# Seven block products in place of eight in three of four rounds of a feed-forward matrix

## The reference

```
x += m @ w_out
x += relu(RMSNorm(x) * g_mlp @ w_up)^2 @ w_down       # w_up 1024 x 4096, w_down 4096 x 1024
y = RMSNorm(x) * g_final                              # the meta tokens are dropped
```

## Time and profile before

| | |
|---|---|
| median of 3 runs | 953.61 us (953.61 to 954.35) |
| the profiled execution, its own time | 954.1 us |
| its span, first to last instruction | 952.3 us |
| TensorE busy | 941.3 us, 7473 matmuls |
| VectorE, ScalarE, GpSimd busy | 535.3, 528.7, 257.3 us |
| mean granted TensorE clock | 0.999 |

### The profile page before, as it was taken

How to read it: one execution, slowest core, us unless ns; L and a number is a source line. 1 busy time by engine, 2 the same in 40 slices (tenths; PEclk the granted TensorE clock), 3 DMA queues, 4 the chain that set the end, 5 groups by cost and what they waited for, 6 DMA issues and landing times.

```text
span 952.3 us, 19721 instructions
## 1 busy us (share of the span) xinstructions
PE 941.3 (99%) x7473; PEld 923.1 (97%) x7473; DVE 535.3 (56%) x915; ACT 528.7 (56%) x826; POOL 257.3 (27%) x188
## 2 busy tenths in 40 slices
PE   8999999999999999999999999999999999999997
PEld 8899999999999999999999999999999999999997
DVE  6479999999999999997653322222111122221133
ACT  6788787878787878786733343333111133331153
POOL 5301010101010101012243444445334244454340
PEclk9999999999999999999999999999999999999999
DMA  6776667676758585768132223234233133243102
GB/s 181 151 175 132 171 125 176 121 180 116 185 109 184 109 181 113 158 144 211 46 110 80 80 85 101 85 93 120 89 88 89 47 88 88 88 121 98 45 23 95
DMA packets 189520, 111.37 MB, mean 117 GB/s; under 512 B 35437, under 2 KB 181277, under 8 KB 189482
## 3 DMA queue, kind: packets, MB, share of 16 engines
q1 hardware_dynamic: 176666, 80.28, 30.6%
q0 software_dynamic: 7632, 27.79, 15.9%
q10 hardware_dynamic: 5184, 2.78, 1.0%
HBM read 75.97 MB, written 7.06 MB: 87 GB/s over the span
## 4 chain that ended last, share of the span: by engine, by line
PE 97%; ACT 1%; DMA 1%; issue 1%; DVE 0%; POOL 0%; DVEq 0%; POOLq 0%
PE dense L551 83%; PE z L671 3%; PE dense L846 3%; PE z L635 2%; PE z L705 2%; DMA w_lo<-w_raw 1%; PE z L565 1%; PE z L639 1%; PE dense L715 0%; PE z L838 0%; PE z L629 0%; PE dense L578 0%; PE z L691 0%; PE z L710 0%; PE z L621 0%
## 5 line engine op out<-in xcount | busy, mean ns | idle before, releaser
L534 POOL TENSOR_TENSOR w_lo<-w_raw,w_hi 128x1024 fp32r<-128x1024 f32 x80 | 192.3, 2406 | 295.0 <-ACT w_hi L939 295.0
L551 PE MATMUL dense<-r_hi,w_hi 128*128 128x272 f32 (+1 forms) x1264 | 263.5, 291 | 1.2 <-DMA w_lo<-w_raw 0.6
L551 PE MATMUL dense<-r_lo,w_hi 128*128 128x272 f32 (+1 forms) x1264 | 262.6, 289 | 0.0
L551 PE MATMUL dense<-r_hi,w_lo 128*128 128x272 f32 (+1 forms) x1264 | 262.2, 289 | 0.0
L939 ACT ACTIVATE w_hi<-w_raw 128x1024 fp32r<-128x1024 f32 x134 | 140.9, 1054 | 113.6 <-PE dense L551 102.6
L551 PEld LDWEIGHTS dense<-r_hi,w_hi 128*128 128x128 f32 x1264 | 198.2, 188 | 1.6 <-DMA w_lo<-w_raw 0.8
L551 PEld LDWEIGHTS dense<-r_lo,w_hi 128*128 128x128 f32 x1264 | 198.8, 188 | 0.7 <-DVE r_lo L1355 0.6
L551 PEld LDWEIGHTS dense<-r_hi,w_lo 128*128 128x128 f32 x1264 | 199.1, 188 | 0.0
L1374 DVE SCALAR_TENSOR_TENSOR acc<-conv_in,cw_cur,acc 128x574 f32<-128x574 f32 x232 | 172.8, 811 | 0.5
L511 POOL DMA_DIRECT2D w_lo<-w_raw x53 | 45.2, 853 | 362.4 <-ACT w_lo L941 362.4
L551 PE MATMUL dense<-s_hi,w_hi 128*128 128x272 f32 x640 | 132.3, 288 | 0.0
(11 more groups left out here) (258 smaller groups left out, 1289.6 us busy)
## 6 DMA issues: line engine op xcount, KB each, us to landing
w_raw<-in_w_in_dram SPq DMA_DIRECT2D x54, 512.0 KB, 5.5
w_lo<-w_raw POOLq DMA_DIRECT2D x53, 512.0 KB, 5.0
w_raw<-in_w_up_dram SPq DMA_DIRECT2D x32, 512.0 KB, 4.0
w_raw<-in_w_down_dram SPq DMA_DIRECT2D x32, 512.0 KB, 3.5
w_raw<-in_w_pw_dram SPq DMA_DIRECT2D x8, 512.0 KB, 3.6
w_raw<-in_w_out_dram SPq DMA_DIRECT2D x8, 512.0 KB, 3.6
x_tok<-in_x_prompt_dram SPq DMA_DIRECT2D x4, 512.0 KB, 6.1
out_dram<-k_blk SPq DMA_DIRECT2D x32, 64.0 KB, 2.4
```

The source lines that it names most:

```text
L534: pool.tensor_tensor(w_lo[:, n], w_raw[:, n], w_hi[:, n].bitcast(F32), ALU.subtract).then_inc(lo_post, 1)
L551: mm = nc.tensor.matmul(out[:, h, 0:half], w[:, wslot, k, :], m[:, k, c0 + h * half:c0 + (h + 1) * half], start=(k == 0 and n == 0), stop= ...
```

## The change

In rounds 0, 1 and 2 the down product of 1024 inner channels by 1024 outputs is made by Strassen's scheme on blocks. Output chunks are taken in pairs (4 pairs a round); inner chunks too: A11, A12, A21, A22 are the quarters of the weights of one pair (even or odd inner chunks, first or second output chunk), B11, B12, B21, B22 those of the activations (even or odd inner chunk, first or second 272 tokens). In place of eight block products there are seven (`SEVEN`), each with 4 inner chunks x 3 passes = 12 matmuls of 272 columns into one bank, with sums of blocks as operands: S1 to S4 of the weights, T1 to T4 of the activations. For that

- the rounds are no longer taken two by two: each has 8 up units and then its down part. Round 3 keeps the plain form, with its up results in `u_hi`, `u_lo`. There are 16 groups in place of 22.
- VectorE makes the sums S1 to S4 (128 x 512 each, in what was `gate_c`), four for each pair of outputs; the first pair's between the up units 5 and 6 of its round, the others between the additions of the pair before.
- ScalarE makes the high parts: of the quarters A11, A12, A22, which it also copies negated into `w_lo`, and of the sums. Each waits until TensorE has finished with the same form of the pair before, for each form has one place in `w_hi` and `w_lo`.
- GpSimd makes the low parts: for the three quarters by an accumulating DMA from `w_raw` (a source of four pieces of 512 B in each partition), for the four sums by a subtraction of 128 x 512.
- the up units of these rounds are turned into seven forms (B11, T1 after an even unit, B21, B22, T2, T3, T4 after an odd one), high parts on ScalarE, sums and low parts on VectorE, in `r_hi`, `r_lo`, `u_hi`, `u_lo`.
- VectorE adds the four bank results x, y, z, w to `xT` in nine additions of 272 columns for each pair (`add_product`). Pairs take `dense` and `z` in turn. TensorE starts product S2 after the addition x11, S3 after x12, A22 after z11.
- SP loads the two blocks of a pair when the pair two before has its low parts and its sums.

```diff
-N_GROUPS = (3 + 2 * ROUNDS) * GROUPS_PER_STAGE
+
+N_SEVEN = ROUNDS - 1
+N_GROUPS = (3 + ROUNDS + 1) * GROUPS_PER_STAGE
+PAIRS = KC // 2
+PRODUCTS = 7
...
+        FORM_HOME = {"A11": (0, 0), "A12": (0, 1), "S1": (1, 0), "S2": (1, 1), "S4": (2, 0), "S3": (2, 1), "A22": (3, 0)}
+        QUARTER_FORMS, SUM_FORMS = ("A11", "A12", "A22"), ("S1", "S2", "S4", "S3")
+        U_FORMS = ("B11", "T1", "B21", "B22", "T2", "T3", "T4")
+        U_SUMS = ("T1", "T2", "T3", "T4")
+        SEVEN = (("A11", "B11", 0, True), ("S1", "T1", 1, True), ("A12", "B21", 2, True), ("S2", "T2", 0, False),
+                 ("S4", "B22", 3, True), ("S3", "T3", 0, False), ("A22", "T4", 2, True))
+        MADE = {w: n + 1 for n, (w, _, _, _) in enumerate(SEVEN)}
+
+        ADDED = {"x11": 1, "z11": 2, "x12": 3, "y12": 4, "w12": 5, "x22": 6, "x21": 7, "y22": 8, "z21": 9}
+        N_ADDED = len(ADDED)
+
+        def form_place(buf, name):
+            slot, h = FORM_HOME[name]
+            return buf[:, slot, h * PAIRS:(h + 1) * PAIRS, :]
+
+        def quarter(P_, name):
+
+            slot = 2 * (P_ % 2) + (name[1] == "2")
+            return w_raw[:, slot].rearrange("p (k t) c -> p t k c", t=2)[:, int(name[2]) - 1]
+
+        def wsum(name):
+            at = OUTTOK + SUM_FORMS.index(name) * PAIRS * P
+            return gate_c[:].rearrange("p k c -> p (k c)")[:, at:at + PAIRS * P].rearrange("p (k c) -> p k c", c=P)
...
+        def u_form(name, m, low=False):
+            n = U_FORMS.index(name)
+            buf = ((r_hi, r_lo), (u_hi, u_lo))[n // 4][low]
+            return buf[:].rearrange("p k c -> p (k c)")[:, ((n % 4) * PAIRS + m) * HALFO:((n % 4) * PAIRS + m + 1) * HALFO]
+
+        def product_bank(P_, n):
+            return z[:, n, 0:HALFO] if P_ % 2 else dense[:, n % 2, n // 2, 0:HALFO]
...
+            def seven_left(P_, b):
+
+                if b == 0:
+                    sync.wait_ge(quarter_lo[0], 16 * (P_ + 1))
+                    sync.wait_ge(quarter_lo[1], 16 * (P_ + 1))
+                else:
+                    sync.wait_ge(quarter_lo[2], 16 * (P_ + 1))
+                sync.wait_ge(wsum_done, len(SUM_FORMS) * (P_ + 1))
...
+                        P_ = PAIRS * rr + p
+                        for b in range(2):
+                            slot = 2 * (p % 2) + b
+                            if p < 2:
+                                sync.wait_ge(lo_post, lows_of_post(g0 + 1, slot))
+                            else:
+                                seven_left(P_ - 2, b)
+                            sync.dma_start(w_raw[:, slot], wdown_v[:, rr, :, 2 * p + b, :]).then_inc(raw_seven[slot], 16)
...
+            def seven_low(P_):
+
+                for name, _ in sorted(MADE.items(), key=lambda item: item[1]):
+                    if name in QUARTER_FORMS:
+                        f = QUARTER_FORMS.index(name)
+                        pool.wait_ge(quarter_hi, len(QUARTER_FORMS) * P_ + f + 1)
+                        pool.dma_start(form_place(w_lo, name).bitcast(F32), quarter(P_, name), accum_op=ALU.add).then_inc(quarter_lo[f], 16)
+                    else:
+                        pool.wait_ge(wsumhi_done, len(SUM_FORMS) * P_ + SUM_FORMS.index(name) + 1)
+                        pool.tensor_tensor(form_place(w_lo, name), wsum(name), form_place(w_hi, name).bitcast(F32), ALU.subtract).then_inc(wsumlo_done, 1)
...
+            def seven(rr, p):
+                P_ = PAIRS * rr + p
+                if p == 0:
+                    for slot in range(2):
+                        claim(slot, X_EMPTIED[slot] + 2 * up_group(rr + 1))
+                if P_ >= 2:
+                    pe.wait_ge(product_added, N_ADDED * (P_ - 1))
+                for name, moving, b, begin in SEVEN:
+                    if name in QUARTER_FORMS:
+                        pe.wait_ge(quarter_lo[QUARTER_FORMS.index(name)], 16 * (P_ + 1))
+                    else:
+                        pe.wait_ge(wsumlo_done, len(SUM_FORMS) * P_ + SUM_FORMS.index(name) + 1)
+
+                    before = {"S2": "x11", "S3": "x12", "A22": "z11"}.get(name)
+                    if before:
+                        pe.wait_ge(product_added, N_ADDED * P_ + ADDED[before])
+                    if p == 0 and name == "A11":
+                        pe.wait_ge(form_ready, form_count(rr, PAIRS - 2, U_FORMS[-1]))
+                    hi, lo = form_place(w_hi, name), form_place(w_lo, name)
+                    for m in range(PAIRS):
+                        if p == 0 and m == PAIRS - 1:
+                            pe.wait_ge(form_ready, form_count(rr, m, moving))
+                        for j, (w, low) in enumerate(((hi, False), (hi, True), (lo, False))):
+                            mm = nc.tensor.matmul(product_bank(P_, b), w[:, m, :], u_form(moving, m, low),
+                                                  start=(begin and m == 0 and j == 0), stop=(m == PAIRS - 1 and j == 2), skip_group_check=True)
+                    mm.then_inc(product_done, 1)
...
+            for rr in range(ROUNDS):
+                g0 = up_group(rr)
+                if rr > 0:
+                    pe.wait_ge(product_added, N_ADDED * (PAIRS * rr - 1))
+                with pe.Fori(g0 + 1 if rr == 0 else g0, g0 + 2) as g:
                     group(g, s_hi, s_lo)
-                with pe.Fori(10 + 8 * rr, 12 + 8 * rr) as g:
-                    group(g, *u_parts[0], (u_ready, 16 * rr + 1))
-                if rr == 0:
-                    with pe.Fori(12, 14) as g:
-                        group(g, *u_parts[1], (u_ready, KC + 1))
-                else:
-                    for f in range(4):
-                        unit(20, f, *u_parts[1], (u_ready, 3 * KC + 1) if f == 0 else None)
-                        if f >= 1:
-                            pe.wait_ge(xg_done, f)
-                            back(f - 1, ((0, 0), (1, 1), (2, 2), (3, 3)))
+                if rr < N_SEVEN:
+                    for p in range(PAIRS):
+                        seven(rr, p)
+            pe.wait_ge(product_added, N_ADDED * PAIRS * N_SEVEN)
+            for f in range(4):
+                unit(LAST_GROUP - 1, f, u_hi, u_lo, (u_ready, 1) if f == 0 else None)
...
+                if rr < N_SEVEN:
+                    m = f // 2
+                    halves = [n32[:, n % 2, h * HALFO:(h + 1) * HALFO] for h in range(2)]
+                    if n % 2 == 0:
+                        nc.scalar.activation(u_form("B11", m), halves[0], ACT.Copy).then_inc(form_hi, 1)
+                        u_sum_high(rr, m, "T1")
+                    else:
+                        nc.scalar.activation(u_form("B21", m), halves[0], ACT.Copy).then_inc(form_hi, 1)
+                        nc.scalar.activation(u_form("B22", m), halves[1], ACT.Copy).then_inc(form_hi, 1)
+                        for name in ("T2", "T3", "T4"):
+                            u_sum_high(rr, m, name)
+                else:
+                    nc.scalar.activation(u_hi[:, f, 0:OUTTOK], n32[:, n % 2, 0:OUTTOK], ACT.Copy).then_inc(uhi_done, 1)
+
+            def u_sum_high(rr, m, name):
+                act.wait_ge(usum_done, usum_count(rr, m, name))
+                nc.scalar.activation(u_form(name, m), usum(name), ACT.Copy).then_inc(form_hi, 1)
...
+            def seven_free(P_, name):
+
+                rr, p = divmod(P_, PAIRS)
+                if p == 0:
+                    act.wait_ge(tile_done, FIRST_POST + 4 * (up_group(rr) + 1) + FORM_HOME[name][0] + 1)
+                else:
+                    act.wait_ge(product_done, PRODUCTS * (P_ - 1) + MADE[name])
+
+            def quarter_high(P_, name):
+                slot = 2 * (P_ % 2) + (name[1] == "2")
+                act.wait_ge(raw_seven[slot], 16 * (P_ // 2 + 1))
+                seven_free(P_, name)
+                nc.scalar.activation(form_place(w_hi, name), quarter(P_, name), ACT.Copy)
+                nc.scalar.activation(form_place(w_lo, name), quarter(P_, name), ACT.Copy, scale=-1.0).then_inc(quarter_hi, 1)
+
+            def wsum_high(P_, name):
+                act.wait_ge(wsum_done, len(SUM_FORMS) * P_ + SUM_FORMS.index(name) + 1)
+                seven_free(P_, name)
+                nc.scalar.activation(form_place(w_hi, name), wsum(name), ACT.Copy).then_inc(wsumhi_done, 1)
...
+                g, P_ = g0 + 1, PAIRS * rr
+                high_post(g, 0)
+                up(g, rr, 4, 0)
+                high_post(g, 1)
+                up(g, rr, 5, 1)
+                if rr < N_SEVEN:
+
+                    quarter_high(P_, "A11")
+                    wsum_high(P_, "S1")
+                    up(g, rr, 6, 2)
+                    quarter_high(P_, "A12")
+                    wsum_high(P_, "S2")
+                    wsum_high(P_, "S4")
+                    wsum_high(P_, "S3")
+                    up(g, rr, 7, 3)
+                    quarter_high(P_, "A22")
+                    for p in range(1, PAIRS):
+                        seven_high(P_ + p)
+
```

(84 more changed lines are left out.)

123 lines of the change are left out of this document (73 added, 50 removed).

## The result

The changed kernel takes 958.94 us (median of 5 runs, 958.48 to 959.65), the kernel before beside it 954.35: ratio 1.0046, 95% interval 1.0035 to 1.0056. By the medians it is 4.6 us slower, where 8 us faster was forecast. The profiled execution took 958.48 us with a span of 956.6.

What follows compares the result with a forecast made beforehand. TensorE, busy in 99% of the span, was taken as the bound. Span 952.3 - 18.0 (matmuls) + 9.9 (three steps) = 944.2, so 945.5 us as median, 0.9% faster; likeliest case 941 to 950, whole range 938 to 962.

Steps and rivals of the forecast that it cites:

- What goes: Down products of three rounds: 144 matmuls less at 124.7 ns each, 18.0 us saved.
- The same bank: New products writing one PSUM bank twelve times running, where two alternated: costs nothing, 125.4 ns for 272 columns.
- Steady pairs: Pair of 10.5 us on TensorE; ScalarE 6.3, VectorE 6.7, GpSimd 8.0 us all stay below it, no waits.
- Rival B: Accumulating transfers of four pieces become the bound in each pair, kernel slower, up to 1008 us; chance 0.18.
- D: Pairs stall inside by 0.3 to 0.5 us, additions waiting behind sums that GpSimd blocks: 950 us; chance 0.09.
- The step: From an up round to the products, three times: stalls of 2.6 to 4.0 us, taken as 3.3, together 9.9.
- Item 1: At the step, the first product waits until the eighth up tile is emptied from its banks: 0.8 us.
- Item 2: Before the step, four weight sums delay emptying tile 7 by 1.7 us; the eighth tile's square starts at 1.2, not 0.8.
- Item 3: At the step, GpSimd's subtractions delay VectorE's first sum to 3.0, x11 to 6.3; S2 lags 1.8 to 3.2 us.
- my upper case: At the step, GpSimd's last subtraction also gets in before VectorE, 1.36 us later: x11 ready at 7.6.
- Items 3 and 4: Transfers at the step, issue 0.86, landing 5.0 us: A12 lands 4.4, needed 3.8; A22 lands 11.6, needed 10.8.
- Rival E: TensorE's clock falls after the stalls, 2.8 us at half speed, 1.4 us a step: 950 us; chance 0.06.

Runs made afterwards that it cites:

- e9: e8 with the next pair's S1, S2, S4 behind z11, x12, y12 in each round's first pair, and second pair's A12 ahead of S1: 945.24 us, ratio 0.9899.
- e2: Changed kernel with GpSimd making only a quarter of the low parts of S4 and S3 in each round's first pair, rest left out: 954.16 us, ratio 0.9988.
- e6: e4 with VectorE adding the first pair's x11 right after emptying the eighth up tile, ahead of its forms: 954.56 us, ratio 0.9995.
- e8: e7 with the first pair's copies on ScalarE reordered and GpSimd following this order: 952.30 us, ratio 0.9962.
- e4: Changed kernel with each output chunk loaded in two transfers, so a quarter is one 2 KB piece per partition, not four of 512 B: 950.97 us, ratio 0.9961.
- e10: e9 with the changed kernel's loads and quarters of four pieces of 512 B again: 949.56 us, ratio 0.9954.
- e3: Changed kernel with small unused matmuls in each round's first pair, 8 before A12 and 14 before S2, keeping TensorE active: 960.04 us, ratio 1.0051.
- e5: e4 with the second slot claimed only ahead of product S1, not before A11: 950.07 us, ratio 0.9945.
- e7: e4 with both the split claim of e5 and the early x11 of e6: 951.75 us, ratio 0.9963.
- e12: e9 with the same order, sums behind the additions, in the second pair of each round as well: 941.12 us, ratio 0.9853.

## Why the prediction was wrong

**What goes: right.** 144 matmuls less at 124.7 ns, 18.0 us. The same bank twelve times costs nothing: 125.5 ns a matmul, as the 125.4 read between the part units.

**Steady pairs: the conclusion right, the sizes not.** Pairs three and four ran through at 10.54 us, so rivals B and D as stated did not happen. Pair two did wait, 2.2 us in all for transfers, where no wait was forecast. But their margin was thinner than I had it. GpSimd's pair is 4 x 1.86 + 3 x 1.41 = 11.7 us of the profile's durations, which overlap in part, and not 8.0; VectorE's sums of raw weights took 1.70 us in the mean and not 0.68, most of it the hold by GpSimd (0.69 in the median).

**The step: the wrong term.** 3.3 us forecast, 7.3 measured (21.8 / 3). Three places were named rightly: claim, A12, x11. The fourth, A22, never waited; the later waits for transfers were in pair two. Product S2 started 5.4, 4.7 and 4.7 us late in the three rounds, where 1.8 to 3.2 was forecast; of the rest of the 7.3, 1.1 is the clock and 0.9 the transfers of pair two. By item, in round 0, with time 0 at 605.7:
- Item 1, 0.8 a step: 1.0 measured.
- Item 2: the four sums were priced free of the lock, 2.7 us. They took 4.6, since GpSimd's subtraction of S1 held the third (the 2.60 above). So the seventh tile came late through ScalarE, and the square of the eighth started at 1.9 and not at 1.2.
- Item 3, the failed one. I had VectorE get in after one of GpSimd's subtractions, at 3.0, or 1.36 later. It waited for all three: its sum ended at 6.7 where I had 3.4, x11 at 9.55 where I had 6.3. The whole difference of 3.3 is there when this sum ends; the eight operations behind it kept their 2.9. It has two parts. About 2.0 come from GpSimd's issue of A12 at 1.4 and not at -0.6: ScalarE's copies of it ended 1.0 late, behind the hold of item 2, and GpSimd began 0.9 after them. These were in none of my cases: the four sums stood in the price without any hold. About 1.3 come from the last subtraction, which VectorE waited for too; that was my upper case (7.6) and not the middle. The rows had shown the hold by single subtractions, and I had VectorE come in between two queued ones. It can (e9), but at the three steps it did not. e2 shows that the subtractions are the cause, e6, e8 and e9 show the same at other places.
- Items 3 and 4, transfers: taken as in the earlier trace rows; with four pieces 1.41 and 5.7 us. Rival B's mechanism was real, below the point from which I had it decide in each pair, but it worked at the step and just behind it: 6.6 us by the starts of the matmuls. The change from four pieces to one is worth 8.0 us in this order (e4) and 4.3 in the best (e9 against e10).
- Rival E, 0.06: the clock did fall, in two of three steps, 1.6 us each, a little more than the 1.4 that the rival had. In the changed kernel this was hidden (e3), in e4 it was not, 1.5 us each time. The stretch of 36 to 42 us on which I set the rival aside was one execution's luck: the clock fell there in 12 of the 14 profiled executions.

The terms of such a step do not add. e2 took 5.3 us of waiting for x11 away and won 4.8 in all with a part of the work left out. e5 mended the claim, e7 the claim and x11, e8 the order as well, and their medians lie within 1.4 us of e4's; only e9 and e12 left no other wait to take the place, and there the clock stayed full too. That queues hide each other I had said for one pair and not for the step.
